# Differences of gate and up's opening rows in other buffers, some of them formed during the output projection

## What is computed

```python
mix = jnp.concatenate([fox_o, dsa_o], axis=-1) @ w_out
h = layer_norm(ALPHA * x + mix, ln1_g, ln1_b)
f = (silu(h @ w_gate) * (h @ w_up)) @ w_down
y = layer_norm(ALPHA * h + f, ln2_g, ln2_b)
```

## Time and profile before

| | before |
|---|---|
| median of 3 runs | 1369.1 us (1366.21 to 1370.1) |
| profiled execution, its own time | 1366.44 us |
| its span | 1364.4 us |
| granted TensorE clock, mean | 0.994 |
| PE busy | 1323.4 us, 97% |
| DVE, ACT, POOL busy | 954.2, 676.6, 539.1 us |

### The profile page before, as it was taken

The page is one execution under the profiler, slowest core; times in us unless marked ns, Lnnn a source line. Parts: engine busy times, 40 slices in busy tenths (PEclk is TensorE's granted clock), DMA queues, the critical chain, the costliest instruction groups (busy, mean ns, idle before and its releaser), DMA issues.

```text
span 1364.4 us, 23638 instructions
## 1 busy us (share of the span) xinstructions
PE 1323.4 (97%) x8882; PEld 1183.3 (87%) x8882; DVE 954.2 (70%) x1802; ACT 676.6 (50%) x1250; POOL 539.1 (40%) x518
## 2 busy tenths in 40 slices
PE   7989999999999999999999999999999999999997
PEld 7859999987776767787799999999999997778886
DVE  4399989888886889668865645555645556576497
ACT  5579979827885888610343222333222333353330
POOL 2506685531332132334555555455555552000011
PEclk9999999999999999999999999999999999999999
DMA  7202432258685622612045344355344359787552
GB/s 238 67 14 69 151 113 76 67 130 198 184 221 115 149 45 38 210 47 70 24 140 178 116 147 155 117 177 178 118 146 155 119 199 340 277 282 246 170 191 102
DMA packets 150369, 197.17 MB, mean 145 GB/s; under 512 B 28120, under 2 KB 106872, under 8 KB 150256
## 3 DMA queue, kind: packets, MB, share of 16 engines
q1 hardware_dynamic: 150256, 195.67, 46.7%
HBM read 136.69 MB, written 48.38 MB: 136 GB/s over the span
## 4 chain that ended last, share of the span: by engine, by line
PE 54%; DVE 2%; POOL 1%; issue 0%; DMA 0%; ACT 0%; POOLq 0%; DVEq 0%; SPq 0%
PE banks L2866 32%; PE banks L2250 6%; PE banks L2964 5%; PE banks L2965 5%; PE banks L2966 5%; PE banks L2982 1%; DVE rows L3355 0%; POOL rows_T L3164 0%; DMA down_raw<-in_w_down 0%; PE banks L2348 0%; PE banks L2346 0%; PE banks L2840 0%; DVE h_B_lo L3258 0%; DVE sample_T L3270 0%; DVE down_lo L3223 0%
## 5 line engine op out<-in xcount | busy, mean ns | idle before, releaser
L3140 POOL TENSOR_TENSOR w_lo<-w_S,w_hi 128x512 fp32r<-128x512 f32 x88 | 119.4, 1357 | 106.4 <-ACT w_hi L3019 106.4
L2866 PE MATMUL banks<-h_T_hi,w_hi 128*128 128x264 f32 x704 | 144.7, 285 | 0.9 <-DVE h_B_lo L3258 0.7
L2866 PE MATMUL banks<-h_T_lo,w_hi 128*128 128x264 f32 x704 | 143.7, 285 | 0.0
L2866 PE MATMUL banks<-h_T_hi,w_lo 128*128 128x264 f32 x704 | 142.9, 283 | 0.0
L3118 ACT CAST down_hi<-down_raw 128x1024 fp32r<-128x1024 f32 x77 | 80.7, 1051 | 122.4 <-PE banks L2966 63.9
L3019 ACT CAST w_hi<-w_S 128x512 fp32r<-128x512 f32 x88 | 54.7, 622 | 168.7 <-PE banks L2866 147.4
L2222 POOL TENSOR_TENSOR ln_rstd<-ln_var_eps,ln_power 128x1 f32<-128x1 f32 (+1 forms) x18 | 25.1, 1394 | 257.8 <-DVE ln_var_eps L2213 136.3
L3223 DVE TENSOR_TENSOR down_lo<-down_raw,down_hi 128x1024 fp32r<-128x1024 f32 x77 | 93.0, 1227 | 44.1 <-ACT down_hi L3118 44.0
L2964 PE MATMUL banks<-down_hi 128*128 128x512 f32 x308 | 120.9, 393 | 0.4 <-DVE rows L3355 0.3
L2966 PE MATMUL banks<-down_hi,down_lo 128*128 128x512 f32 x308 | 120.5, 391 | 0.0
L2965 PE MATMUL banks<-down_lo,down_hi 128*128 128x512 f32 x308 | 120.4, 391 | 0.0
(11 more groups left out here) (418 smaller groups left out, 3785.5 us busy)
## 6 DMA issues: line engine op xcount, KB each, us to landing
down_raw<-down_a SPq DMA_DIRECT2D x77, 256.0 KB, 4.0
gate_raw<-in_w_gate SPq DMA_DIRECT2D x11, 1024.0 KB, 6.6
down_t<-in_w_down SPq DMA_DIRECT2D x44, 256.0 KB, 4.1
down_w<-down_t SPq DMA_DIRECT2D x22, 512.0 KB, 3.4
down_raw<-in_w_down SPq DMA_DIRECT2D x22, 512.0 KB, 6.5
down_raw<-down_w SPq DMA_DIRECT2D x44, 256.0 KB, 4.2
up_raw<-in_w_up SPq DMA_DIRECT2D x10, 1024.0 KB, 6.4
down_a<-down_s SPq DMA_DIRECT2D x10, 1024.0 KB, 4.1
```

What stands on the lines that cost most here:

```text
L2866: mm = nc.tensor.matmul(pp[:, bank[to] + ch, 0:PIECE], l, x[name][:, k, ch * PIECE:(ch + 1) * PIECE], start=opens and k == 0 and i == 0, s ...
L3140: nc.gpsimd.tensor_tensor(w_lo[n % 2][:, :, :], weight(m, SCHEME[q][0]), f32(w_hi[n % 2][:, :, :]), ALU.subtract).then_inc(w_lo_done, 1)
```

## The change

T3 and T4 no longer overwrite T1 and T2 place by place. T3's four tiles go to `other`, `p1`, `u2` and, for the last, T1's fourth buffer; T4's go to `u3` and T1's first three. So T3 has to wait for no transposition except in its last tile, and POOL forms it as soon as the rows are there: (T3, 0) and (T3, 1) inside the projection's loop, (T3, 2) and (T4, 0) ahead of the first `split`, (T4, 1) ahead of the last T1. `ROWS_MADE` counts in the new order. In `LOWERED` the pair (T1, 3), (B21, 2) comes ahead of (T2, 0), (B21, 1), and ACT's third weight cast comes after the copy of (T1, 3) and not ahead of it. The number of instructions is the same; PE's order is not touched.

```diff
                 mix_lo(order_of_places[n + 2])
             if p in (2, 4):
                 first_differences(pool, p // 2 - 1)
+            elif p in (5, 6):
+                plain_differences(pool, p - 5, place_of(p - 1) + 1)
+
+    def plain_differences(pool, j, rows):
+        t = MIX_ORDER[2 * j]
+        pool.wait_ge(h_done, rows)
+        nc.gpsimd.tensor_tensor(t_rows["T3"][j][:, :], rows_out[:, t + 4, 512:D], rows_out[:, t + 4, 0:512], ALU.subtract)\
+            .then_inc(c["rows_made"], 1)
...
-LOWERED = EARLY + [("B11", 3), ("T1", 1), ("T1", 2), ("T1", 0), ("S", "T1"), ("T2", 0), ("B21", 1), ("T1", 3), ("B21", 2),
+LOWERED = EARLY + [("B11", 3), ("T1", 1), ("T1", 2), ("T1", 0), ("S", "T1"), ("T1", 3), ("B21", 2), ("T2", 0), ("B21", 1),
                    ("T2", 1), ("S", "T2"), ("T2", 2), ("B21", 3), ("T2", 3)] + PAIRED[:6] + [("S", "rest")] + PAIRED[6:]
...
+T4_AT = [None, 0, 1, 2]
...
-        t_rows["T3"], t_rows["T4"] = t_rows["T1"], t_rows["T2"]
+        t_rows["T3"] = [other[:, 0:512], p1[:, 0:512], u2[:, 0:512], t_rows["T1"][3]]
+        t_rows["T4"] = [u3[:, 0:512]] + t_rows["T1"][0:3]
...
-                elif x == ("T2", 1):
+                elif x == ("T1", 3):
                     split(2)
...
-                elif name == "T3":
-                    pool.wait_ge(rows_made, max(made("T1", j), made("T2", j)))
-                    pool.wait_ge(h_tr, transposed("T1", j))
                 else:
                     pool.wait_ge(rows_made, made("T2", j))
-                    pool.wait_ge(h_tr, transposed("T2", j))
+                    if T4_AT[j] is not None:
+                        pool.wait_ge(h_tr, transposed("T1", T4_AT[j]))
...
             first_differences(pool, 2)
             differences("T2", 0)
             differences("T2", 1)
+            pool.wait_ge(m_lo, NT + 1)
+            plain_differences(pool, 2, place_of(NT - 3) + 1)
+            differences("T4", 0)
             split(0)
             norm1.root(pool, NT, P, NT)
+            differences("T4", 1)
             first_differences(pool, 3)
             split(1)
             differences("T2", 2)
             differences("T2", 3)
-            differences("T3", 0)
-            differences("T3", 1)
             split(2)
-            differences("T3", 2)
+            last_plain_differences()
             split(3)
-            differences("T3", 3)
-            for j in range(3):
-                differences("T4", j)
+            differences("T4", 2)
             split(4)
             differences("T4", 3)
```

More of the change, by code:

```diff
@@ L2453, in last_rows @@
                                            ALU.add).then_inc(h_done, 1)
-    return sync, tensor, scalar, gpsimd, vector, first_differences
+    return sync, tensor, scalar, gpsimd, vector, first_differences, plain_differences
 NB = D_FF // (2 * P)
@@ L2524 @@
 BANKS.update({(x, j): 7 - j % 2 for x in ("T3", "B22", "T4") for j in range(4)})
-ROWS_MADE = [("T1", 0), ("T1", 1), ("T1", 2), ("T2", 0), ("T2", 1), ("T1", 3), ("T2", 2), ("T2", 3)] + [
-    (x, j) for x in ("T3", "T4") for j in range(4)]
+ROWS_MADE = [("T1", 0), ("T1", 1), ("T3", 0), ("T3", 1), ("T1", 2), ("T2", 0), ("T2", 1), ("T3", 2), ("T4", 0), ("T4", 1), ("T1", 3),
+             ("T2", 2), ("T2", 3), ("T3", 3), ("T4", 2), ("T4", 3)]
+T4_AT = [None, 0, 1, 2]
 def transposed(name, j):
@@ L2563, in mix_and_ffn @@
         c["rows_made"] = sem("rows_made")
-        mix_sync, mix_tensor, mix_scalar, mix_gpsimd, mix_vector, first_differences = mix_out(nc, d, c, sem, pp, t_rows)
+        mix_sync, mix_tensor, mix_scalar, mix_gpsimd, mix_vector, first_differences, plain_differences = mix_out(nc, d, c, sem, pp, t_rows)
         c["loaded_at"] = [x + (0, 0, 0, 0, 0, 80, 64, 0, 0)[i] for i, x in enumerate(c["loaded_at"])]
@@ L3152, in differences @@
                 t = TILE_ORDER[j]
-                left, right = {"T2": (y[:, t + 4, 512:D], t_rows["T1"][j]), "T3": (y[:, t + 4, 512:D], y[:, t + 4, 0:512]),
-                               "T4": (t_rows["T2"][j], y[:, t, 512:D])}[name]
+                left, right = (y[:, t + 4, 512:D], t_rows["T1"][j]) if name == "T2" else (t_rows["T2"][j], y[:, t, 512:D])
                 if name == "T2":
@@ L3157, in differences, with last_plain_differences @@
                     pool.wait_ge(*((pre_done, place_of(NT - 2) + 1) if j < 2 else (h_done, NT + 2)))
-                elif name == "T3":
-                    pool.wait_ge(rows_made, max(made("T1", j), made("T2", j)))
-                    pool.wait_ge(h_tr, transposed("T1", j))
                 else:
                     pool.wait_ge(rows_made, made("T2", j))
-                    pool.wait_ge(h_tr, transposed("T2", j))
+                    if T4_AT[j] is not None:
+                        pool.wait_ge(h_tr, transposed("T1", T4_AT[j]))
                 nc.gpsimd.tensor_tensor(t_rows[name][j][:, :], left[:, :], right[:, :], ALU.subtract).then_inc(rows_made, 1)
+            def last_plain_differences():
+                pool.wait_ge(rows_made, made("T2", 3))
+                pool.wait_ge(h_tr, transposed("T1", 3))
+                plain_differences(pool, 3, NT + 2)
             first_differences(pool, 2)
```

## The result

| | before | after |
|---|---|---|
| median of 7 runs | 1366.63 us (1365.76 to 1370.1) | 1371.16 us (1370.13 to 1372.72) |
| ratio | | 1.0033 by the medians; interval 1.0019 to 1.0042 around 1.003 |
| profiled span, own time | 1364.4, 1366.44 us | 1370.0, 1372.06 us |

Slower by 0.3%, 4.5 us by the medians; the interval runs from 2.6 to 5.7 us. Two executions further down, one of "both late, old low order" (the profiled one, at a mean clock of 0.948) and one of "best order", ran some 80 us longer than the rest and are left out of every median and ratio.

What follows compares the result with a forecast made beforehand. The opening was taken to hang on DVE's queue, not POOL's. Two DVE delays, 0.95 + 0.93, and the new low order brought lateness to 2.8; 1369.1 + 2.8 = 1371.9 us, range 1368.2 to 1375.2.

Steps and rivals of the forecast that it cites:

- (a): (T3, 0) on POOL during the projection's seventh iteration, behind `mT_lo`: cost nothing, with over 4 us of cover.
- (b): (T3, 1) directly behind the loop's last root starts ahead of DVE's L2239, which ends 0.95 late; bounds 0 and 1.28.
- (d): (T4, 1) between the last tile's root and the last T1 makes DVE's L2452 wait 0.93; bounds 0 and 1.28.
- no block: Rival: POOL doesn't get in front of DVE, in one place or both; +0.8 or +1.8, 1369.9 to 1370.9; chance 0.15.
- (c): (T3, 2) and (T4, 0) before `split(0)`: DVE's S1 arrives ahead of (T4, 0); 0 taken, 1.0 if (T4, 0) came first.
- (e): New order of low parts: PE waits 2.4 ahead of (B21, 3), not 0.61; the later 0.70 goes; lateness 2.8.
- the order alone +0.8: New order of low parts without either delay of DVE by POOL: (B21, 1) 1.66 later, 0.9 won back, +0.8.
- 0.5 saved: In the new order of low parts, S2 no longer meets POOL: 0.5 saved, counted in 0.60 from start to start.
- (f): T3 and T4 off POOL's queue later: no PE wait ends on them, the 1.09 and 1.65 waits stay; gain 0.
- is still there: Sign in the changed profile: PE's 1.09 wait on (T3, 1) remains though its rows are some 20 us old.
- a stretch at half clock: Rival: PE's clock halves around 680 behind two long waits, up to 1.7 more; 2.8 + 1.7 = 4.5, 1373.6; chance 0.32.

Runs made afterwards that it cites:

- both late, old low order: After, with (T3, 1) behind (T2, 1), (T4, 1) behind `split(3)`, and before's order of low parts and S2 cast: 1367.93 us, ratio 1.000.
- best order: After, with (T3, 1), (T4, 1) late, (B21, 1) first among low parts, S2 behind the four, (T4, 3) ahead of `split(4)`: 1365.91 us; again 1367.01.
- old low order: After, with before's order of low parts and ACT's cast of S2 in its old place: 1369.16 us, ratio 1.0014, opening 41.00.
- both differences late: After, with (T3, 1) moved behind (T2, 1) and (T4, 1) behind `split(3)`, new order of low parts kept: 1369.18 us, ratio 1.002, opening 41.29.
- the filler: After, with 16 unread identity transpositions on PE ahead of (T2, 1) and 16 ahead of (B21, 3): 1369.44 us, ratio 1.0017; again 1369.27, 1.0013.
- kernel with halves: After, with (T3, 1) formed in two POOL instructions of 256 columns: opening 42.04 us, total not timed.
- low order alone: Before, with only the new order of low parts and the later cast of S2: 1370.03 us, ratio 1.0025, opening 41.25.

## Why the prediction was right, and what it missed

**(a) (T3, 0), cost 0.** Not isolated. It stands where the change put it in every variant made from after, POOL was idle for 4.82 us behind it in after, and the variant with both later differences late and the old low order measured 1.000, so it costs nothing that can be told.

**(b) and (d), the blocks: 0.95 + 0.93 = 1.88.** Right. L2239 read 2.24 (2.2 predicted) and the pair 2.34 (2.3); POOL's half of the change alone lengthened the opening by 1.94, and undoing (b) alone gave back 0.9 to 1.1. The rival "no block", 0.15, is out.

**(c) S1 meets nothing.** Right: 0.74. POOL's (T4, 0) was the one to wait, which cost nothing, as `split(0)` had slack.

**(e) the new low order, up to a lateness of 2.8.** Right for the change as made. Set off by 2.17, the later start of the opening, (B21, 1)'s low part was to end at 682.04 and ended at 682.15, PE was to go on at 682.17 and did at 682.30, and the next half product followed without a wait. The order's own share, on top of POOL's half, is 41.99 or 41.79 less 41.00, 0.8 to 1.0, against 2.8 - 1.88 = 0.92. Wrong in a side result: "the order alone +0.8" without the block holds only if POOL's new queue stays. With both blocks moved away it was 0.9 (39.96, after the stretch is taken off), but with POOL's old queue it was 2.19, since S2 met POOL for 1.48. The "0.5 saved" in (e) needed both halves of the change, as S2 takes 1.19 with POOL's half alone; I had counted it as the order's own.

**(f) nothing gained from T3's early rows.** Right, and the main reading to learn from. With the old low order, the wait that the profile charged to POOL stayed at 1.10 with its rows long made. In after it is split, 0.48 ahead of (T3, 0) and 0.57 ahead of (T3, 1), 1.05 together, both on DVE. The statement that the wait on (T3, 1) "is still there" at 1.09 was thus right in sum and not row by row. The 1.65 ahead of (T4, 0) read 1.64. It did go, to 0.53, once (T4, 3) stood ahead of `split(4)`; the other edits of that kernel were there too, but with both differences late and (T4, 3) in its old place it was still 1.64.

**The total.** The opening was predicted at +2.8 and measured at +2.93 and +2.73. The whole was predicted at +2.8 and measured at +4.5 and +4.3. The weak step is the choice between forecast and rival: I held "a stretch at half clock" to be an alternative with a chance of 0.32, but it came with the forecast, in both profiles of after. The rival's +4.5 is what the medians show; the forecast's +2.8 lies just inside the lower end of one interval and just outside that of the other (2.6 to 5.7 and 2.9 to 6.3 us), so a term of some 1.5 to 1.7 was probably missing from the sum.

What made me discount the rival was 8.57 busy of 11.7 at a clock of 1.00. Yet the waits in that window are all 1.09 or less, and the 1.65 that I named with them lies outside it. The 2.32 wait of the earlier trace rows was the like case, and I overlooked another: in the trace of before PE waits 3.13 us ahead of 97.61, and the clock is at half from inside that wait to 103.2 (timeline of PE, then windows):

```profile
97.61 0.32 PE L899 MATMUL pi<-iT_new 64*32 64x32 f32 x4 [3.13 <-ACT relu L628]
```

```profile
96.30:103.20 6.90, 5.59 (x25) 5.18 (x26) 6.25 (x12) 2.88 (x6) 0.00 (x0) 0.51 0.06 12
```

The Trainium skill, "TensorE: Matmul & The Clock Gate", "What's actually happening", speaks for the discounted side: an idle array falls back to half. The traces agree in part: 3.4 us at 0.50 behind waits of 2.3 in four openings of seven, none in the other three.

That 1371.9 came within 0.8 of 1371.16 is two errors against each other, and so partly luck. The base of 1369.1, a median of three runs, was 2.5 above the median of seven, and the change was 1.7 too small. The three runs spread over 3.9 us and the profiled execution took 1366.44, so the base was uncertain by more than the change that was to be forecast.

**Still open:** where the median loses 4.3 to 4.5 while the profiled opening loses 2.7 to 2.9. The mean granted clocks and the filler, which recovers about as much as is missing, point to the clock, but in no profile of after does the stretch cost that in the opening.

## What to carry to other kernels

Work that is pulled forward on POOL had a price here where DVE's next instruction reads two operands in SBUF, 0.9 us each time: look for what stands directly behind the semaphore that releases both engines. Ask of a wait with several conditions which of them was met last, by the rows, before moving what the profile names. And a long PE wait, 2.3 us here, can cost more than itself, as the clock may fall behind it; matmuls that nobody reads can stand in its place, though an order without the wait was better here (37.3 against 41.8 in the opening).

## What the runs showed of the hardware

- When DVE's L2239 starts 0.13 behind a POOL instruction, it takes longer by POOL's duration less 0.33: excess 0.40, 0.41, 0.96 and 2.07 beside 0.73, 0.74, 1.29 and 2.40 us.
- The two engines took turns. An operation that had waited went next: POOL's (T4, 0) took 1.74, its second half of (T3, 1) 1.71, DVE's S2 1.48 between two differences.
- Operations as short as 64 elements were blocked like large ones. A low part of the sample rows takes 0.21 unblocked (best order, at 692.36). The pair that forms `sample_T`, beside two or more of POOL's differences, took 2.52 before, 1.74 in the kernel with halves and 2.53 in the profile of after (timeline of DVE):

```profile
662.09 2.53 DVE L3282 TENSOR_TENSOR sample_T<-sample_B,sample_T 128x64 f32<-128x64 f32 x2
```

- The granted clock fell to 0.50 for 3.4 us behind single waits of 2.27 to 2.31 us in the opening, and behind one of 1.83 earlier in the profile of after (ahead of 437.86, clock 0.50 from 439.04), though not behind each: 2.30 in the old low order kept 1.00, and so did 3.07 in the low order alone. What decides it is open.
- A stretch of 3.4 us at half clock cost 0 to 0.2 us in the opening where a wait followed that it could eat into, and 1.3 us where it lay over work throughout.
